# Softmax queries and keys in the first two projection passes, transposed a stage later, and three running sequences inside the projection

## The reference

```
gq, gk, gv, gg, glr, dq, dk, dv = split_cols(xn @ w_in)
dq = rms_norm(dq.reshape(B, T, 4, 2, 64), q_gain)
dk = rms_norm(dk.reshape(B, T, 4, 2, 64), k_gain)
```

## Time and profile before

| | us |
|---|---|
| median of 3 runs (1946.66 to 1960.76) | 1950.88 |
| the profiled execution's own time | 1954.16 |
| its span, first to last instruction | 1952.2 |
| `project`, to about | 484 |
| `mixers`, to about | 1081 |
| the later stages | 871 |

### The profile page before, as it was taken

How to read it: one execution, slowest core, us unless ns; L and a number is a source line. 1 busy time by engine, 2 the same in 40 slices (tenths; PEclk the granted TensorE clock), 3 DMA queues, 4 the chain that set the end, 5 groups by cost and what they waited for, 6 DMA issues and landing times. The chain is left out here.

```text
span 1952.2 us, 37190 instructions
## 1 busy us (share of the span) xinstructions
PE 1633.7 (84%) x15031; PEld 1271.2 (65%) x15031; DVE 1284.1 (66%) x1692; ACT 853.6 (44%) x1357; POOL 402.5 (21%) x371
## 2 busy tenths in 40 slices
PE   5879899998478888688889499429999999999990
PEld 3747676786257777456667288417888888888870
DVE  6446442153668787679784554538888888988964
ACT  5331302222022322243434454127877877877850
POOL 0012122100213334233332000041022122222204
PEclk9979999999569999799999699659999999999995
DMA  9539699704858999999999423038999999999957
GB/s 334 183 122 355 230 351 364 253 28 145 332 195 345 384 370 421 365 331 384 364 359 375 140 100 151 22 152 323 397 401 407 409 400 405 404 403 405 402 210 277
DMA packets 109167, 585.71 MB, mean 300 GB/s; under 512 B 15248, under 2 KB 20752, under 8 KB 56048
## 3 DMA queue, kind: packets, MB, share of 16 engines
q0 software_dynamic: 47184, 304.44, 40.9%
q1 hardware_dynamic: 61856, 279.40, 36.6%
HBM read 537.80 MB, written 46.01 MB: 299 GB/s over the span
## 5 line engine op out<-in xcount | busy, mean ns | idle before, releaser
L2222 DVE TENSOR_TENSOR e_l<-first_w,e_h 128x1024 fp32r<-128x1024 f32 x256 | 294.9, 1218 | 10.4 <-ACT e_h L2219 10.1
L2219 ACT CAST e_h<-first_w 128x1024 fp32r<-128x1024 f32 x256 | 250.2, 1048 | 83.1 <-POOLq L2292 42.7
L375 DVE STREAM_TRANSPOSE d_ring<-d_ring 128x2048 f32<-128x2048 f32 x96 | 219.8, 2299 | 16.8 <-DMA d_ring<-in_cache_k,rows 16.3
L2181 PE MATMUL ps<-e_h,e_xh 128*128 128x512 f32 x512 | 207.2, 405 | 3.1 <-DVE e_xl L2231 3.1
L2183 PE MATMUL ps<-e_h,e_xl 128*128 128x512 f32 x512 | 204.2, 399 | 0.0
L2182 PE MATMUL ps<-e_l,e_xh 128*128 128x512 f32 x512 | 204.1, 399 | 0.0
L250 PE MATMUL ps<-d_ring,d_qb 128*32 128x128 f32 x3072 | 118.1, 303 | 87.8 <-DVE d_ring L375 87.4
L632 PE MATMUL ps<-wh,xh 128*128 128x512 f32 (+1 forms) x432 | 183.5, 425 | 6.2 <-DVE wl L867 6.2
L634 PE MATMUL ps<-wh,xl 128*128 128x512 f32 (+1 forms) x432 | 174.5, 404 | 0.0
L633 PE MATMUL ps<-wl,xh 128*128 128x512 f32 (+1 forms) x432 | 174.4, 404 | 0.0
L2299 POOL COPY e_row<-order 128x1 uint32 x32 | 80.7, 2523 | 424.2 <-PE ps L2189 418.1
(11 more groups left out here) (347 smaller groups left out, 3045.0 us busy)
## 6 DMA issues: line engine op xcount, KB each, us to landing
e_w<-in_w_down SPq DMA_DIRECT2D x32, 2048.0 KB, 8.8
first_w<-in_w_up SPq DMA_DIRECT2D x62, 1024.0 KB, 7.7
first_w<-in_w_gate SPq DMA_DIRECT2D x62, 1024.0 KB, 10.6
cat<-in_w_in SPq DMA_DIRECT2D x8, 2048.0 KB, 12.9
ys_d<-e_y SPq DMA_DIRECT2D x32, 512.0 KB, 10.0
ys_d<-cat POOLq DMA_DIRECT2D x1, 8192.0 KB, 32.5
kT<-in_x_prompt SPq DMA_DIRECT2D x8, 512.0 KB, 8.1
m_stage<-in_w_out SPq DMA_DIRECT2D x4, 1024.0 KB, 5.0
```

The costliest lines, as they stand in the source:

```text
L375: dve.transpose(self.in_ring((KEYS, b, g)), self.in_ring((KEYS, b, g))).then_inc(self.s_kt, 1)
L2181: pe.matmul(out, high, w_high, start=first, stop=False)
L2219: return act.copy(h13[:, :, kk, :], w13[:, :, kk, :])
L2222: return dve.tensor_tensor(l13[:, :, kk, :], w13[:, :, kk, :], h13[:, :, kk, :].bitcast(F32), ALU.subtract)
```

## The change

The passes become dq, dk, dv, v, gate, qk, each for all nine tiles. The tiles of x are now prepared inside the dq pass, one tile ahead. Prompt queries and keys stay as rows: the queries go to a new tensor `q_d` in memory, the keys to their output as before. Only tile 0 is transposed in `project` (`turn(0, SC)` and `turn(TILES, SC)`). Three sequences run inside dv, v, gate and qk (104 slots over 108 points), five in `mixers` (168 slots; the softmax schedule still runs to slot 199). In `mixers` SyncE reloads `qk_d` and the key rows (into the space of `qT`), and each key tile is transposed in `turn_prompt_keys`, six slots after the start of its linear step; then the query rows are loaded over it and transposed in four of the slots 92 to 98. The reload of `v_d` moves into the qk pass.

```diff
-EARLY = 2
+EARLY = 3
...
+    PASSES = [(name, EVERY) for name in ("dq", "dk", "dv", "v", "gate", "qk")]
...
+    WOVEN = [u for u, (_, name, _) in enumerate(UNITS) if name in ("dv", "v", "gate", "qk")]
...
@@ project, SyncE
+                    elif name in ("dq", "dk") and (name, i) != ("dq", 0):
...
+                            to = k.q_d[i - 1] if name == "dq" else k_rows[META + P * (i - 1):META + P * i]
+                            sp.dma_start(to, kn[:, n % 2, :]).then_inc(s_ko[n % 2], 16)
...
+                    if (name, i) == ("qk", 1):
...
                         sp.dma_start(k.cat[:, 1:TILES, W:D], k.v_d[1:TILES].rearrange("i p n -> p i n")).then_inc(s_back, 16)
+                r.stored(sp)
...
@@ project, TensorE
-                    if u == 1:
-                        turn_x(1)
-                    if name == "v":
-                        if i + 2 < TILES:
-                            turn_x(i + 2)
-                        elif i == TILES - 1:
+                    if p == 0:
+                        if i + 1 < TILES:
+                            turn_x(i + 1)
+                        else:
                             decays()
...
+                    if (name, i) == ("dq", 2):
+                        turn(0, SC)
...
+                    elif (name, i) == ("dk", 2):
+                        pe.wait_ge(s_sp, 2)
+                        turn(TILES, SC)
+                    elif (name, i) == ("dk", 5):
                         new_scores()
@@ project, ScalarE
+                for i in range(1, TILES):
                     sum_squares(i)
                     high_x(i)
...
+                    if i >= 2:
+                        roots(i - 2)
...
+                    if (name, i) == ("dk", 0):
                         log_sigmoid()
@@ project, VectorE
+                    elif i >= 2:
+                        norm(i - 2)
...
+                norm(7)
+                keep_decays()
+                low_w(1)
+                keep_spread(1)
+                norm(8)
+                finish_decays()
+                page_rows()
                 for i in range(TILES):
+                    if i == TILES - 1:
+                        low_w(2)
+                    norm(TILES + i)
...
@@ mixers, SyncE (between the old states and lam; after lam; after the first sequence's output)
+                sp.dma_start(k.cat[0:T0, 0, 0:W], k.qk_d[0, 0:T0]).then_inc(l_qk[0], 16)
+                sp.dma_start(k.cat[:, 1:5, 0:W], k.qk_d[1:5].rearrange("i p n -> p i n")).then_inc(l_qk[1], 16)
+                sp.dma_start(k.cat[:, 5:TILES, 0:W], k.qk_d[5:TILES].rearrange("i p n -> p i n")).then_inc(l_qk[2], 16)
...
+                sp.dma_start(k.qT[:], k_rows.rearrange("(i p) n -> p i n", p=P)).then_inc(a_k, 16)
...
+                for i in range(TILES - 1):
+                    sp.wait_ge(a_kt, i + 1)
+                    sp.dma_start(k.qT[:, i, :], k.q_d[i]).then_inc(a_q[i % 2], 16)
@@ mixers, TensorE
+                def turn_prompt_keys(i):
+                    pe.wait_ge(a_k, 16)
+                    pe.wait_ge(l_ok, i - 1)
+                    pe.wait_ge(l_end, min(i + 2, TILES))
+                    for h in range(HEADS):
+                        mm = pe.transpose(k.ps[:, LIN_OUT, h * P:(h + 1) * P], k.qT[:, i - 1, h * P:(h + 1) * P], ident)
+                    mm.then_inc(a_kt, 1)
...
                 def linear(n):
+                    if n - lin_at[-1] in (9, 11, 13, 15):
+                        turn_prompt_queries((n - lin_at[-1] - 9) // 2)
@@ mixers, ScalarE
+                def keep_prompt_keys(i):
+                    act.wait_ge(a_kt, i)
+                    act.copy(k.kT[:, :, META + P * (i - 1):META + P * i],
+                             k.ps[:, LIN_OUT, :].rearrange("p (h t) -> p h t", h=HEADS)).then_inc(a_kk, 1)
```

More of the change, by code:

```diff
@@ L492, in project, with rows_stored @@
         q_pad = [pieces[KEPT_P + j].rearrange("p (b h x) -> p b h x", b=SAMPLES // 2, h=HEADS) for j in range(2)]
+        def rows_stored(n, parity):
+            return sum((2 if QK[x] == ("dk", 0) else QK[x][1] > 0) for x in range(n + 1) if x % 2 == parity)
+        squared = k.cat[:, KD, 0:W]
         def slots_at(u, third):
@@ L816, in _ @@
                 high_w(0)
[L817 to L824, removed]
-                for i in range(3, TILES):
+                for i in range(1, TILES):
                     sum_squares(i)
@@ L949, in new_rows, with keep_decays, finish_decays @@
                     chain.link(dve.memset(k.mt, 0.0))
+                def keep_decays():
+                    dve.wait_ge(s_gk, 48)
+                    for i in range(TILES):
+                        n = rows_of(i)
+                        dve.wait_ge(s_z, i + 1)
+                        dve.tensor_tensor(k.z[0:n, i, :], k.ps[0:n, 6 + i % 2, 0:GW], bgk[0:n], ALU.add).then_inc(s_zs, 1)
+                def finish_decays():
+                    dve.wait_ge(s_ln, 2)
+                    for rows, a, b in ((T0, 0, 1), (P, 1, TILES)):
+                        t = log_scratch[0:rows, a * GW:b * GW]
+                        z = k.z[0:rows, a:b, :].rearrange("p a n -> p (a n)")
+                        dve.scalar_tensor_tensor(out=z, in0=z, scalar=0.0, in1=t, op0=ALU.min, op1=ALU.subtract).then_inc(s_log, 1)
                 dve.wait_ge(s_gain, 16)
@@ L1018, in mixers @@
     STEP = [(i, h) for x in range(1, TILES // 2 + 1) for h in range(HEADS) for i in (TILES - x, x)]
+    Q_ORDER = [i for x in range(1, TILES // 2 + 1) for i in (TILES - x, x)]
+    Q_BANK = (5, 6, 5, 6, 6, 7, 6, 7)
     GROUPS_OF = {i: [list(range(0, i + 1))[a:a + 4] for a in range(0, i + 1, 4)] for i in range(1, TILES)}
@@ L1198, in linear_out @@
                         pe.wait_ge(l_end, i + 2)
+                    pe.wait_ge(a_kk, i)
                     if i >= 2:
@@ L1258, in running_linear, with turn_prompt_queries @@
                                 mm.then_inc(h_n, 1)
+                def turn_prompt_keys(i):
[5 more added lines that the diff above has]
+                    mm.then_inc(a_kt, 1)
+                def turn_prompt_queries(x):
+                    for y in (2 * x, 2 * x + 1):
+                        i = Q_ORDER[y]
+                        pe.wait_ge(a_q[(i - 1) % 2], 16 * ((i - 1) // 2 + 1))
+                        if y == 0:
+                            pe.wait_ge(l_m, 4 * (TILES - 1))
+                        elif y == 5:
+                            pe.wait_ge(l_ok, TILES - 1)
+                        if y >= 2 and y != 5:
+                            pe.wait_ge(a_qq, (1, 2, 4, 4, 5, 6)[y - 2])
+                        for h in range(HEADS):
+                            mm = pe.transpose(k.ps[:, Q_BANK[y], h * P:(h + 1) * P], k.qT[:, i - 1, h * P:(h + 1) * P], ident)
+                        mm.then_inc(a_qt, 1)
                 def linear(n):
+                    if n - lin_at[-1] in (9, 11, 13, 15):
+                        turn_prompt_queries((n - lin_at[-1] - 9) // 2)
                     for i in range(TILES):
                         after = n - lin_at[i]
+                        if i and after == 6:
+                            turn_prompt_keys(i)
                         if i == 0:
```

205 lines of the change are left out of this document (77 added, 128 removed).

## The result

The changed kernel takes 1990.0 us (median of 4 runs, 1977.44 to 2002.07) where the kernel before, on the same chip, takes 1950.95 (4 runs, 1946.66 to 1960.76): 1.0192 times as long, 95% interval 1.0114 to 1.0271. Slower, and within the range, at 12 us above the forecast of 1978. The profiled execution of the changed kernel is the shortest of its four, 1977.44 us (span 1975.3), against 1954.16 for the profiled one before. What the two traces can explain is therefore 23 us; the medians differ by 39. In the four runs the time and the granted clock, averaged over the span, go together: 1977.44 us at 0.911, 1984.62 at 0.910, 1995.38 at 0.903 and 2002.07 at 0.899.

The account below looks back on a forecast made before the run. TensorE was taken to bound the projection's woven passes, the DMA engines the mixers from 588 to 795 us. Projection 44 us longer, mixers 17 shorter: 27 more, 1981 against the profiled 1954.2, or 1978 as a median; range 1934 to 2004.

Parts of the forecast that it names:

- dq pass over: Projection's first pass, preparing the x tiles at 7.9 us each: ends at 108, against 125.65 for the tiles' pass now.
- wait for `kn` behind dk 2: In the dk pass TensorE stands 10.7 us for tile 0's normalised keys, behind VectorE's queue of 27.4 us.
- wait for the first keys: TensorE's wait before the woven passes: 7 us (bounds 0 and 11.3), with VectorE late, against 11.3 now.
- weave, without that wait: Woven passes dv to qk: 36 units, 96 gathers and 27.6 us of weight changes and sequence ends, 344 us.
- wait for `lam`: Early in the mixers, VectorE's 12.6 us wait in slot 5 grows by 5.4 for the `qk_d` reload ahead of it.
- mixers to slot 142: Reloads and moved transposes in the mixers, including 4 us for the late last query tile: together 18 us more.
- slot 142 to merge: Mixers' end: 59 us of values, eight softmax steps at 6.7, closing 5; 118 in all against 152.5 now.
- Rival A: Woven slots in the projection are free, TensorE's matmul share hiding slack: 41 us less, 1937; chance 0.10.
- Eight query stores: Query stores in the projection fall where engines are idle and cost nothing; if they landed late, `norm` would wait.
- Rival C: The mixers' eight last softmax steps fall to the low clock, 3.7 us more a step: +30, 2008; chance 0.13.
- B: Mixers stay bound by gathers to their end, so 32 gathers take 85 us with them: -23, 1928; chance 0.08.
- D: The projection's two waits don't come, VectorE's queue being ready in time: 10.7 + 7 less, 1960; chance 0.17.

## Why the prediction was right, and where it was not

| step | predicted | profiled execution |
|---|---|---|
| first product of dq | 22 | 21.0 |
| dq pass over | 108 | 122.1; with the fill late 108.5 |
| wait for `kn` behind dk 2 | 10.7 | 10.3 |
| dk pass | 62 | 63.5 |
| wait for the first keys | 7 | 7.8 |
| weave, without that wait | 344 | 525.67 - 185.54 - 7.83 = 332.3 |
| woven slots apart | 3.30 | 3.31 |
| projection | +44 | +48.0 |
| wait for `lam` | 12.6 + 5.4 = 18.0 | 17.1 |
| mixers to slot 142 | +18 | 455.8 - 444.5 = +11.3 |
| slot 142 to merge | 118 | 120.3 |
| merge | 1108 | 1108.3 |

The mechanism was right in the main: the projection pays TensorE's price for every woven slot, and the mixers give back far less than their gathers. Rival A (free slots) is refuted by the run with two sequences, which measures 50.4 us for 32 slots and a sequence's ends. It was the one for which the Trainium skill spoke, Perfetto Trace Analysis, section "Identifying the Most-Contended Engine"; here the measurement decides against it: the weight loads were indeed only 236 of 345 us busy, and that left no room.

**The step that failed** is "Eight query stores go where the engines are idle: nothing, but if their landing came late, `norm` would wait." They were not idle: GpSimd's 8 MB fill, which the edit left at the second unit, now fell beside the second weights, the constants and these stores, and VectorE's wait of 19 us set the pass back 14. The prediction named who would wait, but put the term at nothing without a row for that moment, neither of what else was in flight nor of what stood ahead of the stores on SyncE's queue.

It was hidden in the sum by a second error. The weave was priced 12 us too long. The run with two sequences confirms the price of the third, so the excess lies in what the weave has with two sequences too. The prediction called all that was left of the old weave, 18.4 us, changes of weights and ends of sequences, and scaled it with the sequences, by one half. But by the traces' lists of waits TensorE stood for 8.8 us of the old weave beside the wait for the first keys, and for 8.0 of the new one, not 13: that is 5 of the 12. The rest was not separated. Two smaller slips changed little: the terms of the wait behind dk 2 give 27.4 - 3 x 5.40 = 11.2, not 10.7, and those of the dq pass 108.6.

In the mixers two terms were off against each other. By slot 6 they stood 11.3 us later, where 5.4 were taken. The wait for `lam` grew by 4.5, close to the forecast; the other 6.5 are a wait that the prediction doesn't name: in slot 4 VectorE needs the first reloaded tile of `qk_d` (561.80 above). The transposes and the reload of the keys cost nothing more up to slot 90, where 3 were taken; the queries cost 3 and not 9.4. Reading `lam` late gave 16 us: nearly the whole wait, with the 12.6 that stood in the kernel before.

So it was luck that the merge came within 1 us of its forecast: 14 us too few in the dq pass and 2 each behind it and behind slot 142 stand against 12 too many in the weave and 7 too many in the mixers up to slot 142. The median lies 12 us above its forecast, which took the profiled execution of before as 3.3 above its median; that of the changed kernel is 12.6 below its own.

Rival C came true in part. The last steps are 6.4 us apart on average, with the clock at its upper level mostly; but in the seven profiled executions with three sequences and this spacing the stretch from slot 156 to the merge took 82 to 92 us as the clock fell for more or fewer of them. By busy time, the last steps of the changed kernel (a stretch of 82) and of the run with the page rows first (92):

```profile
1049.00:1108.00 59.00, 40.73 (x211) 26.45 (x209) 30.23 (x76) 23.30 (x70) 0.00 (x0) 0.85 0.01 3
```

```profile
1044.00:1112.00 68.00, 51.91 (x208) 33.63 (x208) 30.24 (x76) 22.56 (x67) 0.00 (x0) 0.62 0.01 3
```

This is likely part of why runs of the changed kernel spread over 25 us, as their clocks go with their times; how much of the 39 between the medians it makes, profiles of single executions can't say. Rivals B and D did not come: behind slot 142 it was 120 us, not 71, and both waits stood where they were forecast.

## What to carry to other kernels

A moved store is priced by what is in flight at the moment it is issued, on every engine's queue, and by what stands ahead of it on its own: list those transfers with their bytes before calling it hidden. A wait for a small, late load on an in-order engine cost nearly its whole length here (12.3 of 12.6 us and 16.0 of 17.1 came back), and reading the value later was a better mend than loading it earlier, which handed most of the wait to what was pushed back. What is left of a stretch when the known prices are taken off may be waits: look before scaling it. Work moved out of a stage shortens it only as far as the dependent chain that then stands alone, and that chain may also lose TensorE's clock.

## What was not expected of the hardware

- A 256 KB store (`q_d`) issued at 55.6 us, while the engines moved 364 to 383 GB/s, landed about 16 us later, and the issues ahead of it took SyncE 12.4 us where they took 4.1 without the fill; at the mixers' start, reloads of 1 MB took a median of 41.0 us to land, where 2 MB had taken 8.9.
- TensorE with 44 of 60 us busy was granted an average of 0.77 of its clock; with 0.6 us more transposes per slot it was granted 1.00, and finished sooner.
